# Two linear mixers with modulation chunks moved between their input slots, and an output projection in three rounded passes

## The reference

```python
for i in range(2):
    sh1, sc1, g1, sh2, sc2, g2 = split(silu(c) @ ada_w[i] + ada_b[i], 6)   # 1024 x 6144 each
    h = modulate(rmsnorm(x, norm_mix_g[i]), sh1, sc1)
    mix = (gla_mixer, lru_mixer)[i](h)
    x = x + g1 * mix
    x = x + g2 * grouped_moe(modulate(rmsnorm(x, norm_ffn_g[i]), sh2, sc2))
x = rmsnorm(x, final_norm_g)
# gla_mixer ends:  o = rmsnorm(o, norm_g) * silu(g);  return o @ w_out
# lru_mixer ends:  y = hs * gelu(gate_br);            return y @ w_out
# second block:
merged = g_m * (y_m @ w_m) + g_a * (y_a @ w_a) + g_s * (y_s @ w_s)
x = x + mod[2] * (merged @ w_o)
x = x + mod[5] * conv_ffn(modulate_2(rmsnorm_2(x, norm2_g), mod[3], mod[4]))
```

## Time and profile before

| | |
|---|---|
| median of 3 runs | 1840.32 us (1838.58 to 1842.57) |
| profiled execution | 1840.86 us, span 1839.1 us, mean granted clock 0.984 |
| PE busy | 1757.2 us, 96% of the span |
| DVE, ACT busy | 1120.2 us (61%), 738.3 us (40%) |
| moved by DMA | 392.98 MB, mean 214 GB/s |

### The profile page before, as it was taken

One profiled execution on the slowest core, in us unless ns is written; L12 is line 12 of the kernel. 1 busy time (PEld: TensorE's weight loads), 2 busy tenths in 40 slices (PEclk: granted clock), 3 DMA queues, 4 the chain that ended last, 5 costly groups with the idle time before them and its releaser, 6 DMA issues.

```text
span 1839.1 us, 23862 instructions
## 1 busy us (share of the span) xinstructions
PE 1757.2 (96%) x9637; PEld 1395.3 (76%) x9637; DVE 1120.2 (61%) x1626; ACT 738.3 (40%) x967; POOL 0.2 (0%) x4
## 2 busy tenths in 40 slices
PE   5899999999998989999999998999999999999999
PEld 3796777777777857777767776996754877889998
DVE  3663554446886353744447886726865664549887
ACT  3432433335665233333344666333323433034443
POOL 0000000000000000000000000000000000000000
PEclk9999899999999999999999999999999999999999
DMA  9957577767886777677786891334551332445550
GB/s 332 292 184 265 202 275 279 282 276 259 328 311 222 229 256 247 229 276 283 281 322 238 338 349 41 91 116 159 186 181 46 100 107 92 138 167 182 184 178 24
DMA packets 179029, 392.98 MB, mean 214 GB/s; under 512 B 11365, under 2 KB 102232, under 8 KB 162536
## 3 DMA queue, kind: packets, MB, share of 16 engines
q1 hardware_dynamic: 177246, 390.10, 59.7%
q10 hardware_dynamic: 1674, 1.36, 0.2%
HBM read 390.39 MB, written 1.05 MB: 213 GB/s over the span
## 4 chain that ended last, share of the span: by engine, by line
PE 85%; DVE 6%; DMA 4%; ACT 3%; issue 1%; ACTq 0%; SPq 0%; DVEq 0%
PE bank L920 19%; PE bank L948 9%; PE bank L567 9%; PE bank L1359 7%; PE bank L1157 5%; PE bank L745 5%; PE bank L1370 3%; PE bank L932 3%; PE bank L594 3%; PE bank L611 2%; PE bank L703 2%; PE bank L627 2%; PE bank L963 2%; DMA ring<-in_gla_w_in_dram 2%; DMA ring<-in_ada_w_dram 1%; PE bank L1315 1%
## 5 line engine op out<-in xcount | busy, mean ns | idle before, releaser
L2237 DVE TENSOR_TENSOR parts<-ring,parts 128x2048 fp32r<-128x2048 f32 x144 | 329.1, 2291 | 168.3 <-ACT parts L1639 167.3
L920 PE MATMUL bank<-parts 128*128 128x512 f32 x1536 | 369.7, 400 | 9.6 <-DVE parts L2313 4.0
L1639 ACT ACTIVATE parts<-ring 128x2048 fp32r<-128x2048 f32 x144 | 275.2, 1917 | 227.9 <-PE bank L920 161.6
L920 PEld LDWEIGHTS bank<-parts 128*128 128x128 f32 x1536 | 292.9, 193 | 79.2 <-issue 18.3
L1454 ACT ACTIVATE work<-bank 128x256 f32<-128x256 f32 (+3 forms) x223 | 97.5, 446 | 418.6 <-PE bank L703 68.7
L948 PE MATMUL bank<-parts 128*128 128x512 f32 x768 | 179.4, 391 | 3.7 <-DVE parts L2262 3.7
L948 PEld LDWEIGHTS bank<-parts 128*128 128x128 f32 x768 | 143.4, 188 | 36.7 <-DVE parts L2262 4.1
L567 PE MATMUL bank<-hh,ring 128*128 128x256 f32 x640 | 141.2, 380 | 2.7 <-ACT hh L1501 2.4
L567 PEld LDWEIGHTS bank<-hh,ring 128*128 128x128 f32 x640 | 121.0, 190 | 21.6 <-issue 5.5
L1359 PE MATMUL bank<-parts 128*128 128x256 f32 x1056 | 128.6, 283 | 1.4 <-DVE parts L2784 1.4
L1359 PEld LDWEIGHTS bank<-parts 128*128 128x128 f32 x1056 | 127.6, 192 | 2.2 <-issue 2.2
(11 more groups left out here) (308 smaller groups left out, 2367.5 us busy)
## 6 DMA issues: line engine op xcount, KB each, us to landing
ring<-in_moe_w_gate_dram SPq DMA_DIRECT2D x64, 1024.0 KB, 6.3
ring<-in_moe_w_up_dram SPq DMA_DIRECT2D x64, 1024.0 KB, 7.6
ring<-in_moe_w_down_dram SPq DMA_DIRECT2D x64, 1024.0 KB, 6.4
ring<-in_ada_w_dram SPq DMA_DIRECT2D x48, 1024.0 KB, 7.4
ring<-in_w_in_dram SPq DMA_DIRECT2D x32, 1024.0 KB, 5.9
ring<-in_w_mod_dram SPq DMA_DIRECT2D x24, 1024.0 KB, 7.5
ring<-in_w_up_dram SPq DMA_DIRECT2D x22, 1024.0 KB, 5.1
ring<-in_gla_w_in_dram SPq DMA_DIRECT2D x12, 1024.0 KB, 8.4
```

The source lines that it names most:

```text
L920: ins = pe.matmul(bank[:, :], xg[:, a_, k, tile * P:(tile + 1) * P], w[b_][:, j, :], start=k == 0 and n == 0, stop=k == KT - 1 and n == 2)
L1639: act.activation(moe_w[:, n % 3, 0, :], ring[:, g % RING, :], ACT.Identity)\
L2237: dve.tensor_tensor(moe_w[:, n % 3, 1, :], ring[:, (MOE_AT[layer] + AT[key]) % RING, :], moe_w[:, n % 3, 0, :].bitcast(F32), sub).then_inc ...
```

## The change

Three parts.

1. GLA: chunk 8 goes between input slots 10 and 11, in the plan and on PE; on PE the four head norm sums go with it, ahead of input slot 11. ACT takes chunk 8 and does `inverses` ahead of the tanh, and the tanh in two halves; DVE multiplies in two halves, `gla_y` counts to 2.
2. LRU: chunks 6, 7 and 8 go one behind each of the last three input slots. ACT does Exp and Tanh of the recurrence ahead of the copies of tiles 2 and 3; cubic, gelu and the last product are done in two halves; `lru_y` counts to 2.
3. `w_out` runs in three rounded passes. Its four slots become the first of the 37 (`ENDS`) that go through `w_parts`; the merged tiles are rounded by ACT (`merged_high`) and DVE (`merged_low`). ACT's third split waits for all merged lows (that buffer lies over `g_acc`). The splits of slots 3, 4 and 5 stand behind squares 1, 3, 5 on ACT and residuals 1, 3, 5 on DVE.

```diff
-        for chunk in BEFORE_GLA_OUT:
+            if j == 10:
+                yield from mod(*BEFORE_GLA_OUT[0])
+        for chunk in BEFORE_GLA_OUT[1:]:
             yield from mod(*chunk)
...
         for j in range(5, 8):
             yield "lru_in", wide(lin_w, 256 * (j - 4))
+            yield from mod(*WITH_LRU_GATE[j - 5])
...
@@ PE, GLA
             rows_turned(1, ROW_TILES)
-            in_linear(to_act, gla_parts)
+            mod_chunk(*BEFORE_GLA_OUT[0])
             for hd in range(GLA_H):
                 norm_sum([sq[:, j, 0:T] for j in (2 * hd, 2 * hd + 1)], T)
-            for i, chunk in enumerate(BEFORE_GLA_OUT):
+            in_linear(to_act, gla_parts)
+            for i, chunk in enumerate(BEFORE_GLA_OUT[1:]):
                 mod_chunk(*chunk)
-                if i:
-                    mod_turn(7 + i)
+                mod_turn(8 + i)
             mod_turn(11)
-            pe.wait_ge(sem("gla_y"), 1)
+            pe.wait_ge(sem("gla_y"), 2)
...
@@ PE, LRU
-            for j in range(5, 8):
+            for j, chunk in enumerate(WITH_LRU_GATE):
                 linear("lru_in", to_act, h, T)
-            marks["lru_g"] = to_act.n
+                marks["lru_g", j] = to_act.n
+                if j:
+                    mod_turn(17 + j)
+                mod_chunk(*chunk)
             for i, chunk in enumerate(BEFORE_LRU_OUT):
                 mod_chunk(*chunk)
-                if i:
-                    mod_turn(17 + i)
+                mod_turn(20 + i)
             mod_turn(23)
-            pe.wait_ge(sem("lru_y"), 1)
+            pe.wait_ge(sem("lru_y"), 2)
...
@@ PE, w_out
-            pe.wait_ge(sem("merged"), 8)
             for j in range(4):
-                residual_out("w_out", lambda k: g_acc[:, k, :], 2, j)
+                w = split("w_out", KT)
+                for m in range(2):
+                    ps = to_dve.fill(pe)
+                    for k in range(KT):
+                        if j == 0 and m == 0:
+                            pe.wait_ge(sem("merged_low"), k + 1)
+                        for i, (a_, b_) in enumerate(PASSES):
+                            ins = pe.matmul(ps[:, 0:T], w[a_][:, k, m * P:(m + 1) * P], merged_part(b_, k),
+                                            start=k == 0 and i == 0, stop=k == KT - 1 and i == 2)
+                    close(to_dve, ins)
+                    marks["residual", 2, 2 * j + m] = to_dve.n
+                ff_used.append((to_dve.ready, to_dve.n))
...
@@ ACT, GLA
-            a(act.activation(sq[:, :, T:TC], g_g, ACT.Tanh, scale=0.5), sem("gla_tanh"))
+            take_mod()
             inverses(GLA_H, GLA_DV)
-            for j in range(4):
+            a(act.activation(sq[:, 0:4, T:TC], g_g[:, 0:4, :], ACT.Tanh, scale=0.5), sem("gla_tanh"))
+            for j in range(6, 8):
+                take(g_g[:, j, :], done=j == 7 or None)
+            a(act.activation(sq[:, 4:8, T:TC], g_g[:, 4:8, :], ACT.Tanh, scale=0.5), sem("gla_tanh"))
+            for j in range(3):
                 take_mod()
...
@@ ACT, w_out (high(n) rounds slot n of the last 37)
             for n in range(2):
                 high(n)
-            squares(lambda k: f_sq[:, k, 0:T], residual_in(2))
+            for k in range(KT):
+                act.wait_ge(sem("merged"), k + 1)
+                act.activation(merged_high[:, k, :], g_acc[:, k, :], ACT.Identity).then_inc(sem("merged_high"), 1)
+            act.wait_ge(sem("merged_low"), KT)
+            high(2)
+            for k in range(KT):
+                act.wait_ge(*residual_in(2)(k))
+                act.activation(f_sq[:, k, 0:T], x[:, k, :], ACT.Square).then_inc(sem("sq_ready"), 1)
+                if k in (1, 3, 5):
+                    high(3 + k // 2)
...
@@ DVE, LRU
+            cubic(0)
             dve.wait_ge(sem("lru_mult"), 1)
             stt(l_x, l_x, 0.5, l_m, mul, mul)
...
             for j in range(8):
                 v(dve.tensor_tensor_scan(l_h[:, j, :], l_a[:, j, :], l_x[:, j, :], 0.0, mul, add))
+            gated(0)
+            take_mod(*WITH_LRU_GATE[0])
+            cubic(1)
+            take_mod(*WITH_LRU_GATE[1])
+            gated(1)
...
@@ DVE, w_out
+                            if half and j:
+                                low_of_merged(3 + j)
+                    if half and br < 2:
+                        low(br)
+                        for k in (2 * br, 2 * br + 1):
+                            low_of_merged(k)
+            low_of_merged(7)
+            low(2)
+            residual(mods[:, 2, 16:24], after={1: 3, 3: 4, 5: 5}, then=low)
```

More of the change, by code:

```diff
@@ L78 @@
 WITH_LRU_IN = {1: (1, 4), 3: (1, 5)}
-BEFORE_LRU_OUT = [(1, i) for i in range(6, 12)]
+WITH_LRU_GATE = [(1, i) for i in range(6, 9)]
+BEFORE_LRU_OUT = [(1, i) for i in range(9, 12)]
 WITH_HEADS = [(2, i) for i in range(4, 12)]
@@ L452, in build @@
         ff_used = []
-        SPLIT_AT = [(3, 4, None)] + [(3 * i + 2, 3 * i + 3, 3 * i + 4) for i in range(1, FF_PAIRS)]
+        ENDS = 4 + 3 * FF_PAIRS
+        SPLIT_AT = [(7, 8, None)] + [(3 * i + 6, 3 * i + 7, 3 * i + 8) for i in range(1, FF_PAIRS)]
         LOWS = 2 * len(MOE_SPLIT)
@@ L1326, in _ @@
                     linear("branch", to_dve, lambda k: y[:, k, :], T, kt=4, tiles=4)
-            pe.wait_ge(sem("merged"), 8)
-            for j in range(4):
-                residual_out("w_out", lambda k: g_acc[:, k, :], 2, j)
-            norm_sum([f_sq[:, k, 0:T] for k in range(KT)], T, each=sem("sq_ready"))
-            pe.wait_ge(to_dve.taken, to_dve.n)
-            pe.wait_ge(sem("f_zeros"), 1)
-            for b in range(4):
-                pe.matmul(banks[4 + b][:, :], f_zero[:, 0:P], f_zero[:, :], start=True, stop=False,
-                          skip_group_check=True)
-            marks["ff"] = to_act.n
             ff_used.clear()
@@ L1349, in split @@
                 return [w_parts[:, n % 3, o].rearrange("p (k n) -> p k n", k=kt) for o in range(2)]
+            for j in range(4):
+                w = split("w_out", KT)
[10 more added lines that the diff above has]
+                ff_used.append((to_dve.ready, to_dve.n))
+            norm_sum([f_sq[:, k, 0:T] for k in range(KT)], T, each=sem("sq_ready"))
+            pe.wait_ge(to_dve.taken, to_dve.n)
+            pe.wait_ge(sem("f_zeros"), 1)
+            for b in range(4):
+                pe.matmul(banks[4 + b][:, :], f_zero[:, 0:P], f_zero[:, :], start=True, stop=False,
+                          skip_group_check=True)
+            marks["ff"] = to_act.n
             def up(what, first=False):
@@ L1731, in _, with gelu_tanh @@
             a(act.activation(l_m, l_r, ACT.Tanh, scale=-1.0), sem("lru_am"))
-            for j in range(4, 6):
+            for j in range(2, 4):
                 take(l_g[:, j, :])
+            take_mod()
             act.wait_ge(sem("lru_m2"), 1)
             a(act.activation(l_m, l_m, ACT.Sqrt), sem("lru_mult"))
-            for j in range(6, 8):
-                take(l_g[:, j, :])
[L1738 to L1742, removed]
+            def gelu_tanh(half):
+                act.wait_ge(sem("lru_cubic"), half + 1)
+                at = slice(4 * half, 4 * half + 4)
+                a(act.activation(l_r[:, at, :], l_r[:, at, :], ACT.Tanh, scale=0.7978845608028654), sem("lru_gelu"))
+            gelu_tanh(0)
+            for j in range(4, 8):
+                take(l_g[:, j, :])
+                if j == 5:
+                    take_mod()
+            take_mod()
+            gelu_tanh(1)
+            for j in range(3):
                 take_mod()
@@ L2036, in low_in, with residual @@
                         .then_inc(sem("h_low"), 1)
-            def residual(gate):
+            def residual(gate, after={}, then=None):
                 for k in range(KT):
@@ L2043, in residual @@
                                                   in1=x[:, k, :], op0=mul, op1=add))
+                    if k in after:
+                        then(after[k])
             norm(gains[:, 0, :])
@@ L2122, in _ @@
                     stt(o, o, col("gla_norm_g", j), i[:, 0:T], mul, mul)
-                    stt(o, o, 0.5, g_g[:, 2 * hd + j, :], mul, mul,
-                        done=sem("gla_y") if (hd, j) == (3, 1) else s["dve_step"])
-            for chunk in BEFORE_GLA_OUT:
+            for half in range(2):
+                at = slice(4 * half, 4 * half + 4)
+                dve.wait_ge(sem("gla_tanh"), half + 1)
+                stt(g_g[:, at, :], sq[:, at, T:TC], 1.0, g_g[:, at, :], add, mul)
+                stt(g_o[:, at, :], g_o[:, at, :], 0.5, g_g[:, at, :], mul, mul, done=sem("gla_y"))
+                if half == 0:
+                    take_mod(*BEFORE_GLA_OUT[0])
+            for chunk in BEFORE_GLA_OUT[1:]:
                 take_mod(*chunk)
@@ L2786, in _ @@
                     .then_inc(sem("h_split"), 1)
-            low(2)
+            low(6)
             for i in range(FF_PAIRS):
```

64 lines of the change are left out of this document (36 added, 28 removed).

## The result

| | before | changed | ratio |
|---|---|---|---|
| device time, median of 6 runs each | 1839.86 us (1836.74 to 1842.57) | 1830.80 us (1828.00 to 1834.38) | 0.9949 [0.9936, 0.9963] |

The gain is 9.1 us, where 17.8 was forecast. The changed kernel's three means lie within 2 us (1830.9, 1829.6, 1829.2); the kernel before moved more (1839.7 in its first six runs, then 1843.6, 1843.0 and 1842.0). So the gain is best told as about 13 us, and the forecast, which started from the lowest set of the kernel before, missed by some 5 to 9.

What follows compares the result with a forecast made beforehand. The prediction took TensorE (PE), busy for 96% of the span, to bound the kernel. GLA 5.6, LRU 8.0 and `w_out` 4.2 sum to 17.8 us off the profiled 1840.86: forecast 1823, range 1818.5 to 1830.

Steps and rivals of the forecast that it cites:

- GLA, 5.6 forecast: GLA's end: a chunk and norm sums ahead of the last input slot start `gla_out` at 160.5, not 166.1.
- The 0.5 us for small waits: GLA's end: allowance added to PE's work, which ends at 160.0, to put `gla_out` at 160.5.
- LRU, 8.0 forecast: LRU's end: three chunks behind the last input slots start `lru_out` at 683.0, not 691.0; bounds 0 and 10.5 us.
- The 2.75: LRU's end: the last pair of loads and `lru_out`'s first slot land 2.75 us apart.
- The 5.3: LRU's end: the load ahead of the last pair, asked for at 669.3, lands 5.3 us later, at 674.6.
- `w_out`, 4.2 forecast: `w_out`: 192 rounded passes at 0.120 us, 23.04 instead of 27.86 us; gain 4.2 us, bounds 2 and 4.8.
- The delay of the last residuals: End of `w_out`: the last two residuals wait for the third split; x is whole 1.5 us after PE.
- Rival B: The two router stages behind the first edits give back 4 us at half clock: 1827; chance 0.11.
- A: Moved chunks only move the load wait: 3 us in GLA, nothing in LRU, 4.2 in `w_out`: 1833.7; chance 0.13.
- C: ACT and DVE bound the `w_out` stage, and nothing is won there: 1827.3; chance 0.05.
- D: `w_out`: each rounded pass pays its weight load by itself, 0.243 us, 18.8 us more: 1846; chance 0.03.
- E: Whole kernel: the change does nothing, PE waits elsewhere for the same time: 1840; chance 0.02.

Runs made afterwards that it cites:

- the changed kernel's first trace: First of three profiled runs of the kernel with all three parts, no further change; profiled at 1828.32 us.
- the third trace: Trace of the changed kernel, unchanged, measured a third time beside three variants of it: 1826.97 us, 0.9928 of the kernel before.
- the loads made early: Changed kernel with a fourth LRU chunk moved ahead of the gate slots: 1824.02 us, 0.9901; again 1823.35, 0.9907.
- the first two traces: Traces of the unchanged changed kernel: the first profiled at 1828.32 us, the second from the repeat beside its single parts, 1829.99 us.
- two-pass run: Changed kernel with two of three passes in `w_out`, the product of low weights and high activations left out: 1829.88 us, 0.9925.

## Why the prediction was right and where it was wrong

**GLA, 5.6 forecast, 4.3 to 4.8 in the traces.** The order worked as followed: no wait for the inverses, a full clock from 150 to 160, no load late for a chunk, `gla_y` at 158.1 on DVE where 156.9 was forecast, and not late either. The 0.5 us for small waits was too little: PE stands 1.06 us ahead of `gla_out`. By the trace's DMA records the first `w_out` slot was issued at 154.62 (forecast 153.4) and landed at 161.85 (forecast 159.8), 3.98 us behind the load ahead of it, and `gla_out` starts at 161.94. About 1.2 us of the gain are clock, as said above.

**LRU, 8.0 forecast, 5.6 to 6.3. This is the step that failed: when the last loads land.** The prediction took one load that lands 5.3 us after it is asked for, as if the queue were empty, then a pair and `lru_out`'s first slot at 2.75 each. It had them at 674.6, 677.4 and 680.1; the LRU's gates start 6.7 us earlier (623.8 instead of 630.5) in the changed kernel's first trace, so that is 667.9, 670.7 and 673.4. By the DMA records they landed at 669.84, 672.54 and 675.27, 2.0 us later, and let PE go on at 669.88, 672.67 and 675.32. The 2.75 held (2.70 and 2.73). The 5.3 did not: this load was issued at 663.11 (forecast 662.6) and took 6.73, for three loads of the moved chunks stood ahead of it; they had been issued from 653.72 to 656.45 and landed at 661.87, 664.51 and 667.15. PE's waits for `ada_w` sum to 3.9 us. The rest, about 0.5 us, comes behind the last load: 3.5 us to `lru_out`, forecast 2.9, with half the clock on the half chunk (1.94 us instead of 1.06) and the two turns. In the third trace the pair landed where the forecast has it (the last one 89.4 us into the stage, forecast 89.2), and `lru_out`'s first slot came late: 4.26 us behind it instead of 2.75. So which of the two terms is too small differs from run to run; both are loads. With the loads made early the stage gave 10.3. A reading behind this was off too: of the twelve `ada_w` loads in the trace of before only the last six were asked for almost at once (667.13 to 673.83); the six ahead of them went out one by one, some 6.9 us apart.

**`w_out`, 4.2 forecast, 3.6 to 5.5.** The pass costs 0.120 us: 192 take 1596.88 to 1620.85 with one wait of 0.96, 23.0 without it. One wait came where three were forecast; the start is 1.7 us earlier (467.9 us after the second block's first split matmul instead of 469.6) in the third trace, at full clock throughout. The delay of the last residuals, 1.5 us in the forecast, ends beside PE's norm sum and costs at most the 0.03 us between the sum's end (1624.47) and Ln (1624.50). In the first two traces 1.7 us of this gain are given back at half clock inside the mixers. The prediction set two estimates from the Trainium skill, "TensorE: Matmul & The Clock Gate", beside its row. The formula in section "Back-to-back issue gap" (109 ns) is given there for an isolated matmul, and the same section says that a stream with weight loads is spaced otherwise, so it was not the one to use. The rule on the row groups in "What overlaps and what doesn't" gives about 107 + 109 ns, an estimate. This kernel shows 120 ns, so load and matmul overlap here although the row groups are the same.

**The rest of the kernel was taken to stay as it was.** That is the second thing that failed. The sum counted as won what had been lost at half clock inside the edited stages: before has 10.2 us at half clock in the GLA's and the LRU's ends together, the first two traces of the changed kernel 3.4, the third none. In the first two the total did not fall by this (59.0 and 59.2 us, against 58.2): what was saved there turned up again elsewhere, up to 3.4 us of time. In the third it fell by 12.4 us, and this trace is the one with the largest gain, 15.2 us. So the size of this part differs from run to run, and the traces of three runs don't fix its mean. Rival B told this mechanism with a chance of 0.11 and at the wrong place: the second router stage kept its length (66.86 to 66.95, 66.84 before) and the first stayed within 1.1 us of it; the expert stages took it. It deserved a larger chance.

**The rivals.** A is wrong in its main part: half of the six waits for `ada_w` went, where the forecast said four or five, and the LRU's stage gained 6 us and not nothing. C did not happen, but the two-pass run shows that it was 3% away. D fell with the passes of L1364, 0.120 us each. E fell with the result.

**What stays open.** The first set of the kernel before is 2 to 4 us under its later three in mean; nothing here says why, and it makes up 3 us of the miss. Which waits decide where the half clock falls was shown for one kind of place only, the wait ahead of the first expert. Why `lru_out`'s and `gla_out`'s first slots land 2.9 to 4.3 us behind the load ahead of them, and not 2.75, is open.

## What to carry to other kernels

Price a load by what was asked for ahead of it and has not landed yet, not by the latency of a load that had the queue to itself: here the last six `ada_w` loads ahead of `lru_out` landed 2.6 to 2.7 us apart, though they were issued over 12 us, and the `w_out` slots behind them some 3 us apart. Asking for a chunk one position earlier tests the price. Time won at a lowered clock may be given back where PE is busy; leave it out of the sum, and try to fill a wait that stands ahead of a long run of matmuls, with a fill that fits even if the work ahead of it runs at half clock. When PE's work in a stage falls by a sixth, work out the pitch of the other two engines for one slot at once: here it was 5.57 us against 5.76, with each of the two engines standing over 2 us of it for the other.

## What the runs showed that was not expected

Of one program, traced three times, the half-clock time was 45.8 to 59.2 us, and the same half-clock stretch cost 1.6 us or nothing, depending on which side of one wait it fell; in all 22 places without a fill it fell on one of the two sides. Four idle matmuls in a wait of 3.98 us, in two places, went with totals of 35.7 and 45.9 us and with means about 3 us shorter. Taking a third of PE's passes out of `w_out` changed nothing, and its trace has the longest half-clock time of all, 76.4 us.
